# Head norm, first gate tiles and the linear unit's gate tiles in a float32 hybrid block on one Trainium2 core

## The chip, the cores and the metric

One core of a Trainium2 chip runs the whole program. Its engines work side by side and wait for each other by semaphores: TensorE (PE, with its weight loads PEld) multiplies, VectorE (DVE) and ScalarE (ACT) do the elementwise work, GpSimd (POOL) a little of it, SyncE (SP) issues most transfers. The metric is the time of one execution on the device in microseconds (us).

## What is computed

The reference is a hybrid block followed by two more layers, for 512 positions and a width of 1024, in float32. Here only the first block matters. Its mixer normalises x once and feeds the result to four branches and four sets of gates:

```python
h = rms_norm(x, norm_mix)                       # x * rsqrt(mean(x*x)) * w
rw = h @ w_in[rwkv]                             # RWKV branch, a recurrence over positions
o = head_norm(o, 64e-5) * ln_w + ln_b           # per head of 64: subtract mean, divide by deviation
y_rwkv = (o + bonus) * gate
y_lru = h_scan * gelu(gate_in)                  # linear recurrent unit
branch = einsum('bsmw,mwd->bsmd', ys, w_branch)
merged = sum(sigmoid(gate_logits) * branch)
```

## The kernel before, in words

Everything lies transposed: 128 features on the partitions, 512 positions along the row. So a vector of 1024 features is eight tiles of 128x512. A float32 product is made of three fp32r products: each operand is split into a high part (written by ACT) and a low part (the difference, written by DVE). One weight tile of 1024 by 128 makes one output tile in a `proj` of 8 x 3 = 24 matmuls (lines 622 to 624). The raw weight comes by a transfer that SP issues, ACT writes `whi` (line 1328), DVE writes `wlo` (line 2052). There are three raw slots and three split slots (`NRAW`, `NSPL`), and `W.ahead` splits weights up to three tiles ahead of the tile named in `hi(...)` on ACT or `lo(...)` on DVE: `hi("lg", 0)` splits the weights of `lg` tile 3, and that needs `lg` tile 0 to be finished, since it takes that tile's slot.

Each engine has a program of its own, in an order written out by hand; there is no planner. `due(...)` gives the semaphore values to wait for, and an instruction that waits holds up all behind it on its engine. Seven PSUM banks go round in a ring (`bank`, `PS.free`); an eighth, `PL`, takes the small sums.

Stages of the first block, in order: `rw` (RWKV projections, with the norm's root in `km`), `chunks` (the recurrence in 8 chunks), `post` (head norm and output of RWKV), the norm of x once more (`hn`, for all later tiles), `merge(3)` (gate tiles g and branch tiles b of RWKV in turn: g0, g1, b0, g2, b1, ...), `mamba`, `merge(0)`, `lru`, `merge(1)`, `ret`, `merge(2)`, and so on.

In `post`, PE makes for each tile j the head mean (`ym`, line 834), the bonus (`yb`, line 838) and the sum of squares (`yc_sum`, line 829). DVE subtracts the mean (line 2326) and multiplies the bonus (line 2330). ACT squares (line 1522), takes the root (line 1525), DVE inverts it (line 2334), ACT and DVE split it into `VR` (lines 1528 and 2337). Then for each j PE spreads the root (`yv`, line 844) and makes the gate (`yg`, line 848), and DVE makes three operations (lines 2341, 2345, 2348) that end in the output tile Yt[j].

All engines' `end po` comes next. Then `hn`: ACT squares x (line 1338), PE sums it (line 640), ACT takes the root (line 1344), DVE inverts it (line 2067) and scales (line 2075), ACT writes the high parts (line 1352), DVE (line 2061) and for every third tile POOL (line 3114) the low parts. The x tiles had been overwritten by `rw` and `chunks`, so SP loads them again after the recurrence (line 3206). Then `merge(3)`: ACT copies the eight output tiles to `yp` (line 1546), DVE writes their low parts, and PE starts g0.

In `lru`, PE makes eight `lx` tiles with their block products (line 946) and then eight `lg` tiles. ACT runs tanh and exp for all eight tiles (lines 1663 and 1666), then eight roots (line 1670), then `hi("lg", j)` and the gelu of `lg` tile j. DVE runs three operations per tile (lines 2530 to 2536), then for each tile a product and a scan (lines 2540 and 2543), then `lo("lg", j)` (line 2052) and the output product (line 2548).

Of the kernel before, what the change touches and what calls it, by code (L numbers as in the profile page):

```python
# [310 lines left out]
def build(nc, T, known=None):  # L311

    with ExitStack() as ctx:
# [41 lines left out]
        PT, CT, DP, X = sb(ctx, "PT", NPAR), sb(ctx, "CT", NCON), sb(ctx, "DP", 62), sb(ctx, "X", 8 * S)  # L355
# [22 lines left out]
        with ExitStack() as c1:  # L378
            VF, BSF, SG, H2 = sb(c1, "VF", 8 * S), sb(c1, "BS", S), sb(c1, "SG", S), sb(c1, "H2", 1024)
            PC = sb(c1, "PC", 64)  # L380
            VFt, PC3, BSR, H2R = tiles(VF), r3(PC, 8), BSF.bitcast(F32R), H2.bitcast(F32R)
# [17 lines left out]
            with ExitStack() as c2:  # L399
                yc, sqt = tiles(sb(c2, "yc", 8 * S)), tiles(sb(c2, "sqt", 4 * S))  # L400
                G2, VRF = sb(c2, "G2", 1024), sb(c2, "VR", S)
                VRR = VRF.bitcast(F32R)
# [6 lines left out]
        with ExitStack() as c1:  # L409
            rtmp = tiles(sb(c1, "rtmp", 6 * S))  # L410
# [87 lines left out]

        def norm_of(tag, n, buffers, xs, wname, w0, outs, after=()):
            return dict(tag=tag, n=n, sq=buffers[0:2], r=buffers[2], sc=buffers[3:], xs=xs, w=(wname, w0), outs=outs,  # L500
                        after=list(after))

        def lo_key(tag, j):
# [7 lines left out]


        N = {
            "hn": norm_of("hn", 8, rtmp, Xt, "norm_mix", 0, H, ends("po")),
        }

# [88 lines left out]
        def tensor_program(pe):  # L605
# [29 lines left out]
            def ss(nm, j):  # L635
                tag, n = nm["tag"], nm["n"]
                b = bank("ss", tag, hold=True) if j == 0 else PS.slots[PS.at["ss", tag]]
                for s in due("pe", ("act", "sq", tag, j), ("con", "ld")):
                    pe.wait_ge(*s)
                MM(b, C("ones"), nm["sq"][j % 2], start=(j == 0), stop=(j == n - 1)).then_inc(*up("pe", "ss", tag, j))  # L640
                if j == n - 1:
                    PS.let("ss", tag)

# [178 lines left out]
            def post():  # L822
# [3 lines left out]
                def yc_sum(j):  # L826
                    for s in due("pe", ("act", "ysq", j), ("dve", "bs")):
                        pe.wait_ge(*s)
                    MM(PL[0:16, :], C("selsum", 16 * j, 16 * j + 16), sqt[j % 4], start=(j == 0),
                       stop=(j == 7)).then_inc(*up("pe", "ysq", j))  # L830

                for j in range(8):
# [6 lines left out]
                yc_sum(7)  # L839
                for j in range(8):  # L840
                    b = bank("yv", j)
                    for s in due("pe", ("dve", "vr")):
                        pe.wait_ge(*s)
                    MM(b, heads2(j), VRR, start=True, stop=True).then_inc(*up("pe", "yv", j))
# [10 lines left out]
            def merge(m):  # L855
                hn, st = h_of("hn"), "m%d" % m
                tile((st, "g", 0), "w_gate", (m, 0), 8, H, hn)
                for j in range(8):
                    if j < 7:
                        tile((st, "g", j + 1), "w_gate", (m, j + 1), 8, H, hn)  # L860
# [5 lines left out]
            def mamba():  # L866
                hn = h_of("hn")
# [70 lines left out]
            def lru():  # L938
                hn = h_of("hn")
# [18 lines left out]
            def ret():  # L958
                hn = h_of("hn")
# [360 lines left out]
        def scalar_program(act):  # L1320
# [13 lines left out]
            def square(nm, j, *keys):  # L1334
                tag = nm["tag"]
                for need in due("act", *keys, ("pe", "ss", tag, j - 2) if j >= 2 else None):
                    act.wait_ge(*need)
# [708 lines left out]
        def vector_program(dve):  # L2046
# [307 lines left out]
            def merge(m):  # L2354
# [23 lines left out]
                for j in range(8):  # L2378
                    if j < 7:
                        lo(st, "g", j + 1)  # L2380
# [970 lines left out]
```

## Time and profile before

| | us |
|---|---|
| median of three runs | 4041.46 |
| the three runs | 4040.36, 4041.46, 4042.90 |
| the profiled execution, its own time | 4038.73 |
| its span | 4036.9 |

| engine | busy us | share of the span |
|---|---|---|
| PE | 3785.7 | 94% |
| PEld | 3047.2 | 75% |
| DVE | 2170.1 | 54% |
| ACT | 1501.6 | 37% |
| POOL | 108.1 | 3% |

A timeline row gives the start in us, the duration, the engine, the line, the operation, its output and inputs, how many instructions are merged in the row, and in brackets how long the engine had been idle and which instruction released it. A row of the table of stretches gives the busy time of each engine in a stretch of the span, the clock granted to TensorE as a share of full speed (PEclk; 1.00 is 2.4 GHz and 0.50 is 1.2 GHz), and the transfers. One float32 matmul stands in the trace as two records.

### The profile page before, as it was taken

To read this page: it belongs to the slowest core of one execution; us is meant where nothing else is said; L and a number is where in the kernel's file an instruction comes from. 1 tells how busy PE (TensorE), PEld (TensorE's weight loads), DVE (VectorE), ACT (ScalarE), POOL (GpSimd) and SP (SyncE) were. 2 spreads that over 40 slices of the span, in tenths; PEclk is the share of its full clock that TensorE was granted. 3 is DMA by queue.
4 is the path that set the end of the run, shared out by engine and by line. 5 is a ranking of instruction groups with operands and counts; after the bars stand their busy time and mean duration, and the time that the engine had idled before them with its cause. 6 is when DMAs were issued, how large, how long until landed. Compare 5 with 4: busy or idle time off the path is not lost.

```text
span 4036.9 us, 52064 instructions
## 1 busy us (share of the span) xinstructions
PE 3785.7 (94%) x22086; PEld 3047.2 (75%) x22086; DVE 2170.1 (54%) x3218; ACT 1501.6 (37%) x2563; POOL 108.1 (3%) x134
## 2 busy tenths in 40 slices
PE   8888799889899999999989999999999999999998
PEld 6578478776677678777877787888777778878886
DVE  6854536555542457476565544434575554454345
ACT  5733234234322334243355423322433553232233
POOL 0022000100000000000001000000000010000000
PEclk9999899899999999999999999999999999999999
DMA  3100122012231122323300132332332002322322
GB/s 137 58 3 3 43 84 100 32 59 78 84 115 63 63 89 88 97 86 96 109 9 14 48 96 93 98 96 91 90 107 75 1 16 79 97 94 90 103 87 80
DMA packets 90812, 297.52 MB, mean 74 GB/s; under 512 B 10067, under 2 KB 12627, under 8 KB 90196
## 3 DMA queue, kind: packets, MB, share of 16 engines
q1 hardware_dynamic: 88704, 286.50, 22.2%
q10 hardware_dynamic: 1876, 7.71, 0.5%
q8 instruction: 173, 2.83, 0.3%
q14 instruction: 59, 0.48, 0.0%
HBM read 292.07 MB, written 2.10 MB: 73 GB/s over the span
## 4 chain that ended last, share of the span: by engine, by line
PE 81%; DVE 12%; ACT 5%; issue 1%; POOL 1%; DMA 0%; SPq 0%; DVEq 0%; ACTq 0%
PE ps L622 20%; PE ps L623 20%; PE ps L624 20%; PE ps L1173 3%; PE ps L1192 3%; DVE wlo L2052 2%; ACT whi L1328 2%; PE ps L1183 2%; DVE ftm L2087 1%; PE ps L766 1%; PE ps L759 1%; PE ps L657 1%; PE ps L771 1%; PE ps L659 1%; PE ps L658 1%
## 5 line engine op out<-in xcount | busy, mean ns | idle before, releaser
L2052 DVE TENSOR_TENSOR wlo<-wraw,whi 128x1024 fp32r<-128x1024 f32 (+5 forms) x603 | 664.2, 1103 | 1306.6 <-ACT whi L1328 1300.1
L1328 ACT ACTIVATE whi<-wraw 128x1024 fp32r<-128x1024 f32 (+5 forms) x603 | 578.1, 959 | 1308.3 <-PE ps L624 1225.6
L622 PE MATMUL ps<-HH,whi 128*128 128x512 f32 x1816 | 723.9, 399 | 32.3 <-DVE wlo L2052 18.9
L623 PE MATMUL ps<-HL,whi 128*128 128x512 f32 x1816 | 711.1, 392 | 0.0
L624 PE MATMUL ps<-HH,wlo 128*128 128x512 f32 x1816 | 710.8, 391 | 0.0
L622 PEld LDWEIGHTS ps<-HH,whi 128*128 128x128 f32 x1816 | 343.5, 189 | 117.2 <-issue 24.7
L623 PEld LDWEIGHTS ps<-HL,whi 128*128 128x128 f32 x1816 | 343.6, 189 | 76.8 <-issue 6.3
L624 PEld LDWEIGHTS ps<-HH,wlo 128*128 128x128 f32 x1816 | 343.3, 189 | 72.3
L622 PE MATMUL ps<-HBh,whi 128*128 128x512 f32 x752 | 297.7, 396 | 6.8 <-DVE HBl L2615 6.3
L624 PE MATMUL ps<-HBh,wlo 128*128 128x512 f32 x752 | 293.6, 390 | 0.0
L623 PE MATMUL ps<-HBl,whi 128*128 128x512 f32 x752 | 293.5, 390 | 0.0
L622 PEld LDWEIGHTS ps<-HBh,whi 128*128 128x128 f32 x752 | 141.6, 188 | 41.0 <-DVE HBl L2615 8.9
L623 PEld LDWEIGHTS ps<-HBl,whi 128*128 128x128 f32 x752 | 141.6, 188 | 31.2 <-issue 1.9
L624 PEld LDWEIGHTS ps<-HBh,wlo 128*128 128x128 f32 x752 | 141.5, 188 | 29.8
L1173 PE MATMUL ps<-KPALL,ZT 128*128 128x256 f32 (+3 forms) x384 | 140.2, 450 | 22.7 <-DVE VT L2881 7.8
L622 PE MATMUL ps<-act2h,whi 128*128 128x512 f32 x384 | 152.4, 397 | 0.0
L623 PE MATMUL ps<-act2l,whi 128*128 128x512 f32 x384 | 152.2, 396 | 0.0
L624 PE MATMUL ps<-act2h,wlo 128*128 128x512 f32 x384 | 152.2, 396 | 0.0
L2893 DVE TENSOR_REDUCE sm<-ps 128x1 f32<-128x256 f32 (+3 forms) x192 | 87.1, 455 | 101.0 <-PE ps L1175 99.9
L622 PE MATMUL ps<-yph,whi 128*128 128x512 f32 x256 | 99.6, 389 | 0.0
L623 PE MATMUL ps<-ypl,whi 128*128 128x512 f32 x256 | 99.6, 389 | 0.0
L624 PE MATMUL ps<-yph,wlo 128*128 128x512 f32 x256 | 99.6, 389 | 0.0
(639 smaller groups left out, 6498.1 us busy)
## 6 DMA issues: line engine op xcount, KB each, us to landing
wraw<-in_w_ff SPq DMA_DIRECT2D x88, 512.0 KB, 3.5
wraw<-in_w_bg SPq DMA_DIRECT2D x48, 512.0 KB, 3.5
wraw<-in_ffn_up SPq DMA_DIRECT2D x44, 512.0 KB, 3.2
wraw<-in_w_z SPq DMA_DIRECT2D x36, 512.0 KB, 3.2
wraw<-in_w_gate SPq DMA_DIRECT2D x32, 512.0 KB, 3.2
wraw<-in_w_br SPq DMA_DIRECT2D x32, 512.0 KB, 3.3
wraw<-in_w_rw SPq DMA_DIRECT2D x26, 512.0 KB, 3.3
wraw<-in_w_mam SPq DMA_DIRECT2D x24, 512.0 KB, 3.2
```

Of the source, the lines that this page charges most:

```text
L622: MM(b[0:m, :], hi[:, k, c0:c0 + m], x[0], start=(start and k == 0), stop=False)
L623: MM(b[0:m, :], hi[:, k, c0:c0 + m], x[1], start=False, stop=False)
L624: ins = MM(b[0:m, :], lo[:, k, c0:c0 + m], x[0], start=False, stop=(stop and k == n - 1))
L657: MM(b[:, 0:cols], x[0][:, cs], hi[:, k, 0:cols], start=first, stop=False)
L658: MM(b[:, 0:cols], x[1][:, cs], hi[:, k, 0:cols], start=False, stop=False)
L659: ins = MM(b[:, 0:cols], x[0][:, cs], lo[:, k, 0:cols], start=False, stop=end)
L1173: MM(b[:, 0:nk], job["q"](h)[:, qs], job["k"](h)[:, k0:k0 + nk], start=True, stop=False)
L1183: ins = TR(b[:, 128 * kb:128 * kb + 128], job["pb"][i % 3][:, 128 * kb:128 * kb + 128], C("ident"))
L1192: ins = MM(ob[:, 64 * h:64 * h + 64], job["pt"][i % 3][:, 128 * kb:128 * kb + 128], job["v"](h, kb), start=(kb == 0), stop=(kb == nkb - 1))
L1328: ACTV(W.pair_of(n)[0], W.raw_of(n), ACT.Copy).then_inc(*up("act", "whi", n))
L2052: TT(l, W.raw_of(n), h.bitcast(F32), SUB).then_inc(*up("dve", "wlo", n))
L2893: RED(s[:, h:h + 1], PS.of("sc", *key)[:, 0:job["nk"]], AXX, ALU.max, negate=True).then_inc(*(up("dve") if x else up("dve", "mx", *key)))
```

## The change

1. The inverse root of x's norm, which `rw` has in `km`, is turned onto the partitions by four transposes after projection 6 (PE) and copied to four columns of `DP` (DVE). At the start of `post` four products with the identity spread it over a held bank `hr`. The squares, sums, root and inverse of `hn` are gone, and so is POOL's part.
2. DVE scales x (`hn_scale`) and writes the low parts (`hn_lo`) inside the loop of `post` over ym and yb; ACT writes the high parts (`hn_hi`) there.
3. x is loaded again in two halves, the first after chunk 6, the second after chunk 7.
4. PE makes gate tile g0 of `merge(3)` between the two loops of `post`, and g1 inside the second loop, ahead of j = 2. ACT makes both gates' sigmoids before it copies any output tile; DVE writes the low part of output tile j-1 in step j, and splits two weight tiles in steps 1 and 3.
5. The root of the head norm is split in place in `BS` instead of `VR`, and three square buffers do instead of four.
6. In `lru`, gelu is written to the output tile; the first three `hi`/gelu come before the eight roots, `lo` of `lg` stands in DVE's loops (after j = 3 and 7 of the first, after each odd j of the second).

```diff
@@ tensor program
+                    if i == 6:
+                        b = bank("hrt")
+                        for s in due("pe", ("dve", "rc")):
+                            pe.wait_ge(*s)
+                        for c in range(4):
+                            ins = TR(b[:, 16 * c:16 * c + 16], km[0:16, 128 * c:128 * c + 128], C("ident")[0:16, 0:16])
+                        ins.then_inc(*up("pe", "hrt"))
...
+                b = bank("hr", hold=True)
+                for s in due("pe", ("dve", "hrt")):
+                    pe.wait_ge(*s)
+                for c in range(4):
+                    ins = MM(b[:, 128 * c:128 * c + 128], DP[:, 62 + c:63 + c].to_broadcast([128, 128]), C("ident"),
+                             start=True, stop=True)
+                ins.then_inc(*up("pe", "hr"))
...
                 yc_sum(7)
-                for j in range(8):
+                gate_tile(3, 0)
+                PS.let("hr")
+                for j in range(8):
+                    if j == 2:
+                        gate_tile(3, 1)
                     b = bank("yv", j)
...
-                for j in range(8):
-                    ss(N["hn"], j)
-                here("pe", "end", "hn")
@@ scalar program, post and merge
+                    ACTV(sqt[j % 3], yc[j], ACT.Square).then_inc(*up("act", "ysq", j))
+                    if j >= 2:
+                        hn_hi(j - 2)
...
+                hn_hi(6)
+                hn_hi(7)
+                for need in due("act", ("dve", "vri"), ("pe", "yb", 7)):
+                    act.wait_ge(*need)
+                ACTV(BSR[0:16, :], sqt[0][0:16, :], ACT.Copy).then_inc(*up("act", "vrh"))
...
+                if m == 3:
+                    for j in range(2):
+                        hi(st, "g", j)
+                        sigmoid(j)
                 for need in due("act", *ends(before)):
@@ scalar program, lru
+                def gelu(j):
+                    hi("lg", j)
+                    evac(("lg", j), Yt[j], ACT.Gelu_apprx_tanh, ("lgg", j))
+
+                for j in range(3):
+                    gelu(j)
                 for j in range(8):
                     for need in due("act", ("dve", "lt", j)):
                         act.wait_ge(*need)
                     ACTV(lt[j], lt[j], ACT.Sqrt).then_inc(*up("act", "ls", j))
...
+                for j in range(3, 8):
+                    gelu(j)
@@ vector program, rw and post
+                    if j == 5:
...
+                        VCP(DP[:, 62:66], r3(PS.of("hrt")[:, 0:64], 16)[:, :, 0]).then_inc(*up("dve", "hrt"))
...
+                    if j >= 2:
+                        hn_scale(j - 2)
...
+                    if j >= 3:
+                        hn_lo(j - 3)
+                hn_scale(6)
+                hn_scale(7)
+                PS.free(("hr",), ("dve", "sc", "hn", 7))
+                hn_lo(5)
...
                 REC(sqt[0][0:16, :], sqt[0][0:16, :]).then_inc(*up("dve", "vri"))
...
+                hn_lo(6)
+                hn_lo(7)
...
+                TT(BSR[32:48, :], sqt[0][0:16, :], BSF[0:16, :], SUB).then_inc(*up("dve", "vr"))
...
+                    if j:
+                        result_lo(3, j - 1)
+                    if j in (1, 3):
+                        lo("m3", "g", j // 2)
+                result_lo(3, 7)
@@ vector program, lru
                     TS(lt[j], lt[j], 2.0 ** -116, None, MAXOP).then_inc(*up("dve", "lt", j))
+                    if j in (3, 7):
+                        lo("lg", j // 4)
...
                     SCAN(xc[j], ra[j], iu[j], 0.0, MUL, ADD).then_inc(*up("dve", "lh", j))
...
+                    if j % 2:
+                        lo("lg", 2 + j // 2)
+                for j in range(8):
+                    if j >= 6:
+                        lo("lg", j)
+                    for need in due("dve", ("act", "lgg", j), ("dve", "lh", j)):
+                        dve.wait_ge(*need)
+                    TT(Yt[j], xc[j], Yt[j], MUL).then_inc(*up("dve", "ly", j))
@@ sync program
-                    sp.dma_start(X, T["x"]).then_inc(*up("xr", "ld", by=16))
+                    for i in range(2):
+                        for need in due("sp", ("pe", "O", 6 + i)):
+                            sp.wait_ge(*need)
+                        sp.dma_start(X[:, 4 * S * i:4 * S * i + 4 * S],
+                                     T["x"][:, 4 * S * i:4 * S * i + 4 * S]).then_inc(*up("xr%d" % i, "ld", by=16))
```

## Rows read from the trace of the kernel before

**Rows 1.** Table of stretches: the two places, busy us and PEclk.

```profile
441.00:526.00 85.00, 61.98 (x153) 29.82 (x152) 53.17 (x68) 26.83 (x41) 2.53 (x2) 0.80 0.16 62
...
1011.50:1030.00 18.50, 0.15 (x2) 0.15 (x1) 18.03 (x22) 7.35 (x10) 0.00 (x0) 0.63 0.00 0
```

**Rows 2.** Timeline of PE from the head norm to merge tile g2.

```profile
458.25 1.03 PE L829 MATMUL psl<-sqt,CT 128*16 128x512 f32 x2
...
465.15 0.76 PE L844 MATMUL ps<-VR,H 128*128 128x512 f32 x1 [5.87 <-DVE VR L2337]
...
484.88 10.22 PE L640 MATMUL ps<-rtmp,CT 128*128 128x512 f32 x16 [7.77 <-ACT rtmp L1338]
501.54 0.77 PE L622 MATMUL ps<-HH,whi 128*128 128x512 f32 x1 [6.43 <-DVE HL L2061]
...
525.97 0.39 PE L622 MATMUL ps<-HH,whi 128*128 128x512 f32 x1
```

**Rows 3.** Timeline of DVE in the same stretch.

```profile
454.60 0.69 DVE L2326 SCALAR_TENSOR_TENSOR yc<-ps,YS 128x512 f32<-128x512 f32 x1 [0.17 <-PE ps L834]
...
456.84 0.69 DVE L2326 SCALAR_TENSOR_TENSOR yc<-ps,YS 128x512 f32<-128x512 f32 x1 [0.17 <-PE ps L834]
...
460.22 3.34 DVE L2334 RECIPROCAL sqt<-sqt 16x512 f32<-16x512 f32 x1 [1.31 <-ACT sqt L1525]
...
476.75 0.69 DVE L2348 TENSOR_TENSOR YS<-yc,ps 128x512 f32<-128x512 f32 x1
...
478.92 0.69 DVE L2348 TENSOR_TENSOR YS<-yc,ps 128x512 f32<-128x512 f32 x1
...
503.36 1.41 DVE L2075 SCALAR_TENSOR_TENSOR rtmp<-X,PT,rtmp 128x512 f32<-128x512 f32 x2
...
514.72 4.91 DVE L2061 TENSOR_TENSOR ypl<-YS,yph 128x512 fp32r<-128x512 f32 x8 [0.74 <-ACT yph L1546]
```

**Rows 4.** Timeline of ACT in the same stretch.

```profile
458.22 1.28 ACT L1525 ACT_TABLE_LOAD   x1
459.51 0.68 ACT L1525 ACTIVATE sqt<-psl,DP 16x512 f32<-16x512 f32 x1
...
521.10 1.05 ACT L1328 ACTIVATE whi<-wraw 128x1024 fp32r<-128x1024 f32 x1
522.04 0.59 ACT L1358 ACTIVATE ga<-ps 128x512 f32<-128x512 f32 x1
```

**Rows 5.** Timeline of PE in the mamba stage: the forms nearest to the added ones.

```profile
733.05 0.39 PE L876 MATMUL ps<-CT,AC 16*128 16x16 f32 x4
...
740.04 3.74 PE L899 MATMUL ps<-AC,CT 128*128 128x128 f32 x32
```

**Rows 6.** Timeline of PE in the linear unit: the wait ahead of lg tile 3.

```profile
1029.88 0.77 PE L622 MATMUL ps<-HH,whi 128*128 128x512 f32 x1 [18.35 <-DVE wlo L2052]
```

**Rows 7.** Timeline of ACT in the linear unit.

```profile
1007.48 1.28 ACT L1670 ACT_TABLE_LOAD   x1
...
1037.32 1.06 ACT L1328 ACTIVATE whi<-wraw 128x1024 fp32r<-128x1024 f32 x1 [17.07 <-PE ps L624]
...
1059.08 1.06 ACT L1328 ACTIVATE whi<-wraw 128x1024 fp32r<-128x1024 f32 x1 [3.89 <-PE ps L624]
```

**Rows 8.** Timeline of DVE in the linear unit.

```profile
1005.38 0.43 DVE L2536 TENSOR_SCALAR ltt<-ltt 128x512 f32<-128x512 f32 x1
...
1014.50 1.22 DVE L2543 TENSOR_TENSOR_SCAN lxc<-lra,liu 128x512 f32<-128x512 f32 x1
...
1028.53 1.20 DVE L2052 TENSOR_TENSOR wlo<-wraw,whi 128x1024 fp32r<-128x1024 f32 x1
```

**Rows 9.** Table of stretches: the clock across two idle times of PE.

```profile
459.00:465.00 6.00, 0.28 (x1) 0.00 (x0) 4.01 (x2) 1.80 (x3) 0.00 (x0) 0.86 0.00 0
...
985.00:990.00 5.00, 1.84 (x5) 0.53 (x3) 3.56 (x5) 2.99 (x4) 0.00 (x0) 0.90 0.28 93
```

**Rows 10.** Transfers from 400 to 560 us: issue, KB, us to landing.

```profile
X<-in_x SPq DMA_DIRECT2D x1, 2048.0 KB, 8.7
```

More of the change, by code:

```diff
@@ L398, in build @@
                     NC_, Xj, P1, RS, ST, STn = (sb(c2, n, 512) for n in ("NCc", "Xj", "P1", "RSs", "ST", "STn"))
[L399 to L402, printed above, removed]
+            sb(c1, "below", 51 * S)
+            VF, BSF, SG, H2 = sb(c1, "VF", 8 * S), sb(c1, "BS", S), sb(c1, "SG", S), sb(c1, "H2", 1024)
+            PC = sb(c1, "PC", 64)
+            VFt, PC3, BSR, H2R = tiles(VF), r3(PC, 8), BSF.bitcast(F32R), H2.bitcast(F32R)
+        with ExitStack() as c1:
+            sb(c1, "below", 16 * S)
+            rtmp, G2, sqt = tiles(sb(c1, "rtmp", 4 * S)), sb(c1, "G2", 1024), tiles(sb(c1, "sqt", 3 * S))
+            sb(c1, "below", 18 * S)
+            yc = tiles(sb(c1, "yc", 8 * S))
         def heads2(j):
@@ L1332, in hi @@
                     split_hi(n)
[L1334 to L1337, printed above, removed]
-                ACTV(nm["sq"][j % 2], nm["xs"][j], ACT.Square).then_inc(*up("act", "sq", tag, j))
-            def root(nm):
-                tag, n = nm["tag"], nm["n"]
-                for need in due("act", ("pe", "ss", tag, n - 1), ("dve", "dp")):
-                    act.wait_ge(*need)
-                ACTV(nm["r"], PS.of("ss", tag), ACT.Sqrt, scale=1.0 / (128 * n), bias=EPSC).then_inc(*up("act", "rt", tag))
-                PS.free(("ss", tag), ("act", "rt", tag))
-            def scaled_hi(nm):
-                for j in range(nm["n"]):
-                    sc = nm["sc"]
-                    for need in due("act", ("dve", "sc", nm["tag"], j)):
-                        act.wait_ge(*need)
-                    ACTV(nm["outs"][j][0], sc[j % len(sc)], ACT.Copy).then_inc(*up("act", "hi", nm["tag"], j))
             def evac(key, dst, fn, mark, rows=128, cols=S, **kw):
@@ L1549, in merge @@
                              scale=P("ssm_norm", j)).then_inc(*up("act", "hi", st, j))
-                def sigmoid(j):
-                    for need in due("act", ("dve", "ga" if m == 3 else "mt", st, j - 2) if j >= 2 else None):
-                        act.wait_ge(*need)
-                    evac((st, "g", j), ga[j % 2], ACT.Sigmoid, ("ga", st, j))
-                hi(st, "g", 0)
-                sigmoid(0)
+                if m != 3:
+                    hi(st, "g", 0)
+                    sigmoid(0)
                 if m == 0:
@@ L1568, in merge @@
                 for j in range(8):
-                    if j < 7:
+                    if j < 7 and (m != 3 or j):
                         hi(st, "g", j + 1)
@@ L1670, in lru @@
                     ACTV(lt[j], lt[j], ACT.Sqrt).then_inc(*up("act", "ls", j))
-                for j in range(8):
-                    hi("lg", j)
-                    for need in due("act", ("dve", "lh", j)):
-                        act.wait_ge(*need)
-                    evac(("lg", j), lt[j], ACT.Gelu_apprx_tanh, ("lgg", j))
+                for j in range(3, 8):
+                    gelu(j)
                 here("act", "end", "lr")
@@ L2020, in scalar_program @@
             post()
-            merge(3, "hn")
+            merge(3, "ch")
             mamba()
@@ L3155, in gpsimd_program @@
             here("pool", "end", "po")
-            scaled(N["hn"])
-            here("pool", "end", "hn")
             here("pool", "end", "m3")
```

126 lines of the change are left out of this document (45 added, 81 removed).

## The prediction

> **What bounds the kernel now.** The page comes first: PE is busy 94% of the span, so whatever saves time must close an idle time of PE or take work off it. The table of stretches says where PE is idle. From 441 to 526 us it is busy for 61.98 of 85 us and runs at 0.80 of its clock; from 1011.5 to 1030 it is busy for 0.15 of 18.5 us while DVE is busy for 18.03 [rows 1]. The timelines then say what it waits for. In the first stretch the last sum of squares starts at 458.25, the head root's spread at 465.15 after 5.87 us idle, the sums of the norm of x at 484.88 after 7.77, gate tile g0 at 501.54 after 6.43; g0, g1 and b0 follow, and g2 starts at 525.97 [rows 2]. In the second, PE has done `lg` tiles 0 to 2 and waits 18.35 us for the `wlo` of tile 3 [rows 6], which stands behind ACT's eight roots and DVE's eight scans, though nothing in it needs them. So two marks are enough for the sum: the start of g2 in `merge(3)`, and the end of `lg` tile 7 at 1059.08, where ACT is released for its next split [rows 7]. Behind each PE runs tile after tile, so a shift of the mark is a shift of the end.
>
> **Small added work.** Four transposes stand in the projections of `rw`, where PE is dense: the same form, four in a row, takes 0.39 us with its tail [rows 5]; bounds 0.1 and 0.4, taken 0.3. DVE's copy of four columns hides in DVE's slack there; if it did not, it would cost less than the shortest DVE row, 0.43 [rows 8]. The spread of the root stands on the path, ahead of the first head mean: four float32 products are eight records, and 32 records of the same form take 3.74 us [rows 5], so 8/32 of that, 0.9 us (to 1.8 at the lower clock).
>
> **Post, first loop.** Before, PE sets the pace: the subtractions of the mean start at 454.60 and 456.84, 2.24 apart [rows 3]. After, DVE has four operations per step from j = 3 on: mean 0.61, scale 0.67 (two in a row take 1.41, less the tail of 0.74), bonus 0.61, low part 0.61 (eight in a row take 4.91) [rows 3], together 2.5. DVE becomes the bound by 0.25 a step, 1.1 us up to the last mean, which then starts at 456.84 + 0.9 + 1.1 = 458.9. From its start on, the mean, three scales, a bonus and two low parts take 4 x 0.61 + 3 x 0.67 = 4.4 us: 463.3. ACT meanwhile squares (0.6, as the sigmoid of the same size [rows 4]), makes a high part (0.6), loads its table (1.28) and takes the root (0.68) [rows 4]: 459.6 + 3.2 = 462.8. So the inverse starts at 463.3 instead of at 460.22, and takes 3.34 [rows 3]: 466.7. The low parts 6 and 7 (1.3) and the low part of the root (0.7) follow: the root is ready at 468.7, against some 465.0 before (PE takes it up at 465.15 [rows 2]). **This loop costs 3.7 us.** In it g0 runs: PE is free at 461.3, and its last three products start when the last low part is there, at 468.0, so g0 ends at 468.8, just as the root is ready. It costs nothing.
>
> **Post, second loop.** DVE starts at about 469.5. A step costs 2.17 us (478.92 less 476.75 [rows 3]); after steps 0 and 1 it is 473.8. Now comes the new wait. DVE's low part of output tile 0 needs ACT's high part, and ACT stands in the sigmoid of g1 first. PE does two steps' products (2.2 us) and then g1. A tile takes (1059.08 - 1037.32) / 4 = 5.44 us [rows 7], so g1 ends at 476.5; ACT splits a weight (0.94 to the next start) and does the sigmoid (about 0.5) [rows 4] and the copy (0.6): 478.7. DVE is idle 4.9 us, and queued behind it are all its outputs, so PE's branch tile b0 waits too. From 478.7: eight low parts (4.9), six steps (13.0), two weight splits (2.3): 499. The last product group of b0 takes 1.3 us at the lower clock: **g2 starts at 500.4, not at 525.97**: 25.6 us earlier. The next tile starts at the lower clock, though. In the linear unit the first tile after the wait took 1037.32 - 1029.88 = 7.44 us, 2.0 more than the others [rows 6, 7]; before, g0 paid that. Less 2.0 here and the 0.3 in `rw`: 23.3 us.
>
> **The x loads.** SP has two transfers instead of one, and behind them on its queue only the weights of `merge(3)`, which go out after chunk 7 as before. The whole 2048 KB landed 8.7 us after the issue [rows 10]. The second half goes out as `post` begins, at about 441, and is needed at about 456 by the scale of tile 4: hidden with 7 us in hand. The first half runs beside chunk 7.
>
> **Linear unit.** ACT is free at 1007.48 [rows 7]. It splits the weight of `lg` 3 by 1008.5. DVE asks for it after j = 3, at 1005.8 [rows 8], and waits 2.7 us; `wlo` is there at 1009.8, before PE has ended tile 2 at 1011.5 (1029.88 less 18.35 [rows 6]). The 18.35 us are gone. What is late next is `lg` 4: DVE does four tiles of three operations, 2.0 each (from 1005.8 to the product ahead of the first scan, at 1013.8 [rows 8]), then the split of 1.2: 1019.0, against the end of tile 3 at 1017.0. PE waits 2.0 us. Then DVE needs two scans with their products and one split per tile: (1028.53 - 1014.50 + 0.6) / 8 = 1.83 each [rows 8], so 3.7 + 1.2 = 4.9, under PE's 5.44. Tiles 4 to 7 run through, and tile 7 ends at 1019.0 + 4 x 5.44 = 1040.8. The three gelus ahead of the roots add a table load on ACT, 1.28 [rows 4]; the roots end at about 1018.8, in step with DVE, and gelus 3 to 7 then run beside the tiles. The mark moves from 1059.08 to 1040.8: 18.3 us. If the 2 us of waiting bring the clock down, 1 to 2 us are lost: I take 0.8. **17.5 us.**
>
> **Sum.** 23.3 + 17.5 = 40.8 us. The profiled execution took 4038.73 (span 4036.9), which gives 3997.9 for one like it; the median stands 2.7 above it, at 4041.46, which gives 4000.7. I take 4001.
>
> **A rule weighed.** Around ACT's change of function the trace shows the load at 458.22 for 1.28 us and the root at 459.51, with nothing between [rows 4]. The Trainium skill, page ScalarE: Activation LUTs, section What ACT_TABLE_LOAD costs, gives a drain of about 1380 ns beside a load of about 1283 ns. By that page the head root would be ready 0.9 us later than DVE is, and the sum would be an estimated 0.9 us smaller; the row shows the load alone, and I go by the row.
>
> **Rivals.**
> - *The lower clock through the output loop.* In the idle time that began at 459.3 [rows 2], PE's clock was halved for the last 1.7 of six us (a mean of 0.86), and in the one that began at about 986.8 (1.84 us of work behind 985) for the last 1.0 of five (0.90) [rows 9]: idle for 4 us, and for 2. After the change PE waits about 2 us inside g0. If it falls there and stays low, g0 takes 2.7 us longer, the first two steps' products 2.2 and g1 5.4, and the whole chain through ACT's sigmoid with them: about 10 us, 4011. Against it: g1 is dense, and the tile after the linear unit's wait lost 2.0 us only [rows 6, 7]. The Trainium skill, page TensorE: Matmul & The Clock Gate, Part 1, says that the throttled state is the default and activity releases it; by that rule this loss is real but short.
> - *DVE in the first loop doesn't overlap with ACT.* If each low part waits for its high part, 0.6 us and the signals around it, the loop costs up to 8 x 0.7 = 5.6 us more: 4006. Against it: each low part comes a whole step after its high part is asked for.
> - *The linear unit's gain goes to a new wait.* If DVE's stall for `lg` 3 and the five later splits fall behind the tiles, each tile waits. At one more us a tile it is 5 us: 4006.
> - *Slower.* The second half of x lands late: the scale of tile 4 waits for it, and DVE, in order, holds the whole of `post`. The price is its landing less 456; from a landing at about 497 on, 56 us behind its issue, the change makes the kernel slower. The whole of x took 8.7 us [rows 10], so a half should take 4.4; at the 62 GB/s that the stretch averaged [rows 1] it takes 17 and costs 2 us; it would have to take thirteen times the row's. At fifteen times, 66 us, it is 51 us late: 4052.
> - *It does not do what it says*: the root of `rw` is the same quantity, and both moved pieces of work have no input that comes later, so I give this no more than the 2% for no change, in which both new waits (DVE behind g1, PE behind `lg` 4) would have to eat all.
>
> **How the numbers follow.** The sum with its terms within their bounds, 3993 to 4006: 0.80. The lower clock, 4011 with 4006 to 4016: 0.10. DVE or the linear unit losing more, alone or together, to 4016: 0.05. No change 0.02, slower 0.03. The range of 8 in 10, with the added work at its bounds and the lower clock taken in at its low end: 3992 to 4013. What a measurement of this kernel can tell from no change is about 0.2%, 8 us, so faster means under 4033: 0.95; same 0.02; slower 0.03.
>
> **What would show it.** In the trace of after: POOL's part gone; PE's first output product at about 469 and the split of `lg` 4 as PE's only wait in the linear unit, of about 2 us; an idle time of DVE of about 5 us ahead of the low part of output tile 0, released by ACT; g2 of `merge(3)` some 60 us behind the start of `post` at 441 instead of 85. Wrong would be: a PE clock of 0.5 through g1, a wait for the x load, a DVE step in the first loop above 2.7 us, or more than 3 us of waiting between `lg` tiles.

## The result and the profile after

The changed kernel took 3995.25 us (median of 4 runs, 3992.37 to 3996.56), the one before 4040.91 (4 runs, 4037.0 to 4042.9): a ratio of 0.9887, 95% interval 0.987 to 0.9904, 45.7 us less. The prediction was 4001 with a range of 3992 to 4013, faster. The profiled execution took 3995.15 with a span of 3993.3, so it stands in the middle of its runs; the one of before, 4038.73, stood 2.2 below its median.

The two places first, as a table of stretches (us of the stretch, busy us of PE, PEld, DVE, ACT and POOL with their instructions, PEclk, DMA share, GB/s):

```profile
441.00:459.00 18.00, 16.54 (x38) 4.37 (x37) 16.21 (x26) 8.51 (x14) 0.00 (x0) 1.00 0.37 154
459.00:480.00 21.00, 18.20 (x67) 12.17 (x66) 14.94 (x19) 9.47 (x13) 0.00 (x0) 1.00 0.00 1
480.00:500.00 20.00, 13.96 (x34) 7.78 (x33) 17.04 (x25) 3.97 (x7) 0.00 (x0) 0.73 0.15 52
500.00:526.00 26.00, 26.00 (x110) 21.35 (x109) 7.85 (x8) 6.08 (x7) 0.00 (x0) 0.94 0.24 81
970.00:990.00 20.00, 18.76 (x83) 15.20 (x81) 15.85 (x26) 19.71 (x30) 0.00 (x0) 1.00 0.07 26
990.00:1010.00 20.00, 18.86 (x77) 15.51 (x77) 19.73 (x21) 7.60 (x10) 0.00 (x0) 0.91 0.31 106
```

Where [rows 1] had 61.98 busy us in 85, at 0.80 of the clock, PE is now busy for 48.70 of 59 us up to 500, and dense from there on. POOL has no part left in `post`. Most of what is still idle stands in the third row, at 0.73 of the clock. In the linear unit the empty stretch of 18.5 us is gone.

The timeline of PE in the first place (start, us, engine, line, out<-in, idle time before it and what ended it) answers to [rows 2]:

```profile
439.19 1.13 PE L824 MATMUL ps<-CT,DP 128*128 128x128 f32 x8 [0.79 <-ACT YS L1491]
...
459.68 0.50 PE L612 MATMUL ps<-HH,whi 128*128 128x512 f32 x1
...
465.63 0.50 PE L612 MATMUL ps<-HH,whi 128*128 128x512 f32 x1 [1.57 <-DVE HL L2053]
...
467.13 0.39 PE L843 MATMUL ps<-BS,H 128*128 128x512 f32 x1
...
468.91 0.80 PE L612 MATMUL ps<-HH,whi 128*128 128x512 f32 x1
...
494.02 0.50 PE L612 MATMUL ps<-yph,whi 128*128 128x512 f32 x1 [1.70 <-DVE ypl L2053]
...
496.79 0.79 PE L612 MATMUL ps<-yph,whi 128*128 128x512 f32 x1 [1.79 <-DVE ypl L2053]
...
499.51 0.63 PE L612 MATMUL ps<-HH,whi 128*128 128x512 f32 x1
```

The spread of the root opens `post`, g0 begins at 459.68 and is ended by three late products, the first output product follows at 467.13 without a wait, g1 begins at 468.91, and g2 starts at 499.51, 60.3 us behind the opening instead of 85.3. At the end b0 takes its last low parts one by one, and the clock falls: the products of 0.39 us take 0.63.

DVE's timeline answers to [rows 3]:

```profile
449.95 0.68 DVE L2312 SCALAR_TENSOR_TENSOR yc<-ps,YS 128x512 f32<-128x512 f32 x1
...
452.41 0.68 DVE L2312 SCALAR_TENSOR_TENSOR yc<-ps,YS 128x512 f32<-128x512 f32 x1
...
461.70 3.33 DVE L2328 RECIPROCAL sqt<-sqt 16x512 f32<-16x512 f32 x1
464.96 1.21 DVE L2053 TENSOR_TENSOR HL<-rtmp,HH 128x512 fp32r<-128x512 f32 x2
466.20 0.68 DVE L2333 TENSOR_TENSOR BS<-sqt,BS 16x512 fp32r<-16x512 f32 x1
...
471.30 0.69 DVE L2344 TENSOR_TENSOR YS<-yc,ps 128x512 f32<-128x512 f32 x1
477.15 0.69 DVE L2053 TENSOR_TENSOR ypl<-YS,yph 128x512 fp32r<-128x512 f32 x1 [5.17 <-ACT yph L1539]
...
496.05 1.47 DVE L2053 TENSOR_TENSOR ypl<-YS,yph 128x512 fp32r<-128x512 f32 x2
```

A step of the first loop takes 2.46 us from j = 4 on and DVE is not idle in it: DVE is the bound. The inverse has no wait in front of it any more (1.31 us before). Then there is the new wait of 5.17 us, released by ACT's high part of output tile 0. ACT's timeline shows why it came late, and its table load answers to [rows 4]:

```profile
459.34 1.28 ACT L1513 ACT_TABLE_LOAD   x1
460.64 0.68 ACT L1513 ACTIVATE sqt<-psl,DP 16x512 f32<-16x512 f32 x1
...
475.06 1.06 ACT L1328 ACTIVATE whi<-wraw 128x1024 fp32r<-128x1024 f32 x1 [4.70 <-PE ps L614]
476.02 0.58 ACT L1338 ACTIVATE ga<-ps 128x512 f32<-128x512 f32 x1
476.50 1.14 ACT L1539 ACTIVATE yph<-YS 128x512 fp32r<-128x512 f32 x2
```

ACT is idle for 4.70 us until g1 has ended, splits a weight, does g1's sigmoid, and only then copies output tiles 0 and 1, of which the second had been there since 472.0. In the linear unit PE's, ACT's and DVE's timelines answer to [rows 6 to 8]:

```profile
991.14 0.76 PE L612 MATMUL ps<-HH,whi 128*128 128x512 f32 x1 [2.38 <-ACT ltt L1665]
...
998.21 0.39 PE L612 MATMUL ps<-HH,whi 128*128 128x512 f32 x1
```

```profile
998.47 1.06 ACT L1328 ACTIVATE whi<-wraw 128x1024 fp32r<-128x1024 f32 x1 [4.58 <-PE ps L614]
...
1003.91 1.06 ACT L1328 ACTIVATE whi<-wraw 128x1024 fp32r<-128x1024 f32 x1 [3.90 <-PE ps L614]
...
1014.79 1.06 ACT L1328 ACTIVATE whi<-wraw 128x1024 fp32r<-128x1024 f32 x1 [3.90 <-PE ps L614]
```

```profile
980.71 1.23 DVE L2044 TENSOR_TENSOR wlo<-wraw,whi 128x1024 fp32r<-128x1024 f32 x1 [2.63 <-ACT whi L1328]
...
989.78 1.22 DVE L2044 TENSOR_TENSOR wlo<-wraw,whi 128x1024 fp32r<-128x1024 f32 x1
```

PE's only wait there is the 2.38 us ahead of `lg` 4. The profile names ACT's roots as its releaser, but these had ended at 991.03 and nothing of theirs enters the tile; the last thing the tile needs is DVE's `wlo`, which ends at 991.00. From its first product to that of `lg` 5, `lg` 4 then takes 998.21 - 991.14 = 7.07 us instead of 5.44, which is 1.6 us more. (ACT's splits, at 998.47 and 1003.91, stand at the ends of tiles, 0.26 us behind the next tile's first product.)

**The span in five stages.** All kernels were cut at the same five marks: the first gram product of the chunks, PE's first product of `post`, tile b1 of `merge(3)`, the last block product of the linear unit, and the first product in `ret` that is not part of a projection tile (line 965 of before and after). So "linear unit" also holds `merge(1)` and the first tiles of `ret`, which are the same in all kernels. The columns "post" and "linear unit" hold the change; the three others hold the same instructions in every kernel, and "untouched" is their sum (with the stretch ahead of the chunks left out, 203.5 us in before and 203.7 in after).

| kernel | chunks | post | middle | linear unit | rest | untouched |
|---|---|---|---|---|---|---|
| before | 237.2 | 90.7 | 462.0 | 163.3 | 2880.2 | 3579.4 |
| before_again | 235.8 | 89.5 | 461.0 | 163.3 | 2880.9 | 3577.7 |
| after | 235.5 | 67.4 | 459.1 | 146.8 | 2880.8 | 3575.4 |
| control | 235.6 | 66.1 | 461.1 | 146.8 | 2878.1 | 3574.8 |
| lru_only | 239.2 | 90.9 | 462.0 | 146.9 | 2875.3 | 3576.5 |
| post_only | 235.5 | 66.0 | 457.7 | 164.4 | 2882.2 | 3575.4 |
| root_only | 235.5 | 63.5 | 460.0 | 164.2 | 2874.9 | 3570.4 |
| root_lru | 235.7 | 63.5 | 460.1 | 146.9 | 2881.4 | 3577.2 |
| order_g1 | 237.8 | 61.9 | 459.3 | 146.6 | 2880.7 | 3577.8 |
| g0_within | 235.6 | 57.7 | 459.8 | 146.7 | 2877.8 | 3573.2 |
| x_whole | 235.7 | 66.2 | 461.0 | 146.9 | 2878.7 | 3575.4 |
| lulo_only | 235.0 | 64.7 | 461.2 | 142.7 | 2878.7 | 3574.9 |
| g0_lulo | 235.5 | 57.6 | 461.5 | 143.2 | 2880.7 | 3577.7 |

The change saved 23.3 us in `post` and 16.5 in the linear unit, 39.8 together. The untouched stages vary by several us from one trace to the next, in both directions, and so between kernels whose medians are compared. That is why each experiment below is read from the stage that it touches first, and from its median second. A stage is not free of this either: `post` holds the same instructions in after, control, post_only, x_whole and lulo_only, and took 67.4, 66.1, 66.0, 66.2 and 64.7 us. The start of g2, one tile before the end of that stage, repeats better: 60.3, 60.1, 60.3, 60.0 and 59.2 us behind the opening. The linear unit repeats within 0.3 us (146.6 to 146.9).

### The profile page after: what moved, and what is told of

It reads as the page before. It is cut to its first block, busy times and chain, and to the rows that moved or that the text cites. A ratio compares the mean times of both kernels' runs of the same rounds, so it can differ in the third digit from the quotient of the medians.

```text
span 3993.3 us, 52039 instructions
## 1 busy us (share of the span) xinstructions
PE 3773.1 (94%) x22082; PEld 3043.1 (76%) x22082; DVE 2163.7 (54%) x3219; ACT 1497.0 (37%) x2555; POOL 104.9 (3%) x132
## 4 chain that ended last, share of the span: by engine, by line
PE 81%; DVE 12%; ACT 5%; issue 1%; POOL 1%; DMA 0%; SPq 0%; DVEq 0%; ACTq 0%; POOLq 0%
PE ps L612 20%; PE ps L614 20%; PE ps L613 20%; PE ps L1173 3%; PE ps L1192 3%; DVE wlo L2044 2%; ACT whi L1328 2%; PE ps L1183 2%; DVE ftm L2060 1%; PE ps L754 1%; PE ps L638 1%; PE ps L747 1%; PE ps L759 1%; PE ps L640 1%; PE ps L639 1%
```

## The experiments

My theory: two independent gains, `post` some 23 us and the linear unit some 17, and what remains is set by DVE's order (the wait behind g1). The rivals: the gains are of another size or depend on one another; gate tiles in `post` are what brings the gain, or only the early root; the x load sets something; and the rest of the 45.7 us is not the change at all.

### One half at a time

`lru_only` is the kernel before with the linear unit of the change; `post_only` is the change with the linear unit of before. The diff is that part of the change's own diff; its core:

```diff
-                for j in range(8):
-                    hi("lg", j)
-                    for need in due("act", ("dve", "lh", j)):
-                        act.wait_ge(*need)
-                    evac(("lg", j), lt[j], ACT.Gelu_apprx_tanh, ("lgg", j))
+                for j in range(3, 8):
+                    gelu(j)
```

> The kernel before with the change in the linear unit alone (gelu to the output tiles, the first three ahead of the roots, the low parts of the weights in DVE's loops). Theory: the two places are independent, and this one moves the end of lg tile 7 by 18.35 us of waiting less 2.4 us of new waiting ahead of lg tile 4, so 16.5 us faster than before, 4024 (ratio 0.996). Rival: the 45.7 us of the whole change owe several us to the places of the half-clock stretches in other stages (chunks, mamba), and each half of the change brings such us too; then this one gives 19 or more or 13 or less.

> The changed kernel with the linear unit as it was before. Theory: 24 to 27 us faster than before, 4015 (ratio 0.994), and its gain and that of the linear unit alone add up to that of the whole, 45.7 us. Rival: the sum of both falls short of the whole by more than 3 us, and the rest is not owed to the waits taken away.

Measured: `lru_only` 4019.49 us beside 4039.19 of before, ratio 0.9955 (0.9942 to 0.9967), 19.7 less; `post_only` 4019.26, ratio 0.9954 (0.9941 to 0.9968), 19.9 less. By the medians both expectations missed, and both came out on the side of the rivals: `lru_only` gained over 19, and the two halves together 39.6, which is 6.1 short of the 45.7. By the stages they came out as the theory had them. In the table the stage that each touches is that of the full change (146.9 and 146.8; 66.0 and 66.1 in `control`) and the other is that of before, so the gains are independent: 16.5 and 24.7, 41.2 together, against 39.8 for the change. The medians put the halves nearly level: `post_only`'s runs lie widely apart (4011.35 to 4020.80) and its profiled one was the shortest, and `lru_only`'s untouched stages were 2.9 us shorter than those of before. I read the halves by the stages; why the whole beats the sum of the medians is not shown.

### The early root without the gate tiles

`root_only` is `post_only` with g0 and g1 back where every other merge has them, behind the output loop, on all engines:

```diff
-                gate_tile(3, 0)
                 PS.let("hr")
                 for j in range(8):
-                    if j == 2:
-                        gate_tile(3, 1)
                     b = bank("yv", j)
...
-                if m != 3:
-                    gate_tile(m, 0)
+                gate_tile(m, 0)
...
-                    if j in (1, 3):
-                        lo("m3", "g", j // 2)
                 result_lo(3, 7)
```

> As the run before, and gate tiles g0 and g1 of merge 3 go back behind the loops (their sigmoids behind the copies of the output tiles, DVE's weight splits behind its low parts): the early root alone. Theory: DVE sets the pace of the output loop at 2.78 us a step and has no wait of 5.2 us and no weight splits in it, so it ends near 489; g0 and g1 then run beside its end and behind it, and g2 starts 3 us later than with the gates within: 21 to 22 us faster than before, 4019. Rival: the gates within are worth the two tiles that they take out of the way, 10.9 us, and the root alone gives 14 us, 4027.

Measured: 4011.79 us, ratio 0.9933 (0.9921 to 0.9945): faster than `post_only`, where I had expected slower. `root_lru`, the same edit on the full change, was run beside the change itself (`control`, its exact copy):

> The changed kernel as it is, for comparison on one chip with the three that follow. Theory: 0.9885 of the kernel before, some 45 us faster; g2 of merge 3 starts 60 us behind the first product of the output stage's start, whatever the length of the stages ahead of it. Rival (the clock's share): the stages that the change does not touch differ by several us between two executions of this same kernel, since the stretches at half clock lie elsewhere; then the mark in the trace repeats within 0.5 us and the total does not within 2 us.

> The changed kernel with gate tiles g0 and g1 of merge 3 back behind the output loop (as in the root alone, with the linear unit's change). Theory, from the traces of the root alone: g1 inside the output loop holds up DVE by 5.2 us and two weight splits by 2.3 more, while behind the loop g0 and g1 are hidden by DVE's own tail, three steps of it; so this is 2.6 to 3.9 us faster than the changed kernel up to branch tile b1, 3991. Rival: the 7.5 us between the medians of the two earlier runs are real, and it is 7 to 8 us faster, 3987.

Measured: `control` 3993.50, ratio 0.9887 (0.9871 to 0.9902), which repeats the ratio of the change, and its g2 starts 60.1 us behind the opening; `root_lru` 3991.62, ratio 0.9881 (0.9863 to 0.9898). Both pairs agree in the stage: 63.5 against 66.0 and 66.1, so b1 starts 2.6 us earlier with the gate tiles outside. The medians of the first pair lie 7.5 us apart, those of the second 1.9. The profiled spans of the first (4009.6 and 4001.8) are 7.8 apart, of which `post` has 2.6, the rest stage 7.3 (2882.2 and 2874.9) and the middle -2.3: most of it isn't the edit. So **the two gate tiles within `post`, as the change places them, gain nothing and cost some us**. How many is not sharp: against 63.5 in both kernels without them stand 64.7 to 67.4 in the five traces with them, and g2 starts 59.2 to 60.3 us behind the opening instead of 58.1; the runs of the second pair overlap. The whole gain of the first place comes from the rest, that is from the early root and the scaling of x moved into the loop. PE's timeline of `root_only` shows all its waits from 462 to 512 us:

```profile
467.00 0.76 PE L840 MATMUL ps<-BS,H 128*128 128x512 f32 x1 [7.28 <-DVE BS L2320]
...
478.02 0.49 PE L840 MATMUL ps<-BS,H 128*128 128x512 f32 x1 [0.38 <-DVE YS L2331]
479.28 1.12 PE L844 MATMUL ps<-SG,G 128*128 128x512 f32 x2 [0.77 <-DVE yc L2324]
480.79 0.50 PE L612 MATMUL ps<-HH,whi 128*128 128x512 f32 x1 [0.38 <-DVE YS L2331]
```

PE waits 7.28 us for the root, but DVE then goes through its outputs with waits of 0.95 and 0.24 us in the first step alone. DVE has three outputs and four low parts more to do when PE has finished the last output product; PE does g0 and g1 in that time, from 480.79 on, and b0 finds its low parts ready. I had expected g2 3 us later than in the change, which is at some 502.5; it started at 497.24. The two tiles fit beside DVE's tail, and I had let part of them stand behind it. In the change the tiles save PE's time, of which there is enough, and cost DVE's, of which there is none: 5.2 us of wait and two splits of 1.15 us each.

### The order around g1

`order_g1` keeps both tiles within and lets ACT copy outputs 0 and 1 before it turns to g1; PE does g1 one step later:

```diff
-                    if j == 2:
+                    if j == 3:
                         gate_tile(3, 1)
...
-                    for j in range(2):
-                        hi(st, "g", j)
-                        sigmoid(j)
+                    hi(st, "g", 0)
+                    sigmoid(0)
...
                         ACTV(yp[j][0], Yt[j], ACT.Copy).then_inc(*up("act", "hi", st, j))
+                        if m == 3 and j == 1:
+                            hi(st, "g", 1)
+                            sigmoid(1)
```

> The changed kernel with two places exchanged: ACT copies output tiles 0 and 1 ahead of the split and sigmoid of gate tile g1, and PE makes g1 ahead of output step 3 instead of 2. Theory: DVE's wait of 5.2 us for the copy of output tile 0 is on the path of b0 and goes away with nothing in its place, 4 to 5 us faster than the changed kernel, 3991, 50 us faster than before. Rival: the wait comes back at the next output step, where DVE waits for the products that stand behind g1 on PE, and nothing or under 2 us is gained, 3994 to 3995.

Measured: 3989.35 us, ratio 0.9881 (0.9868 to 0.9895), against 3993.5 to 3995.3 for the change, which was measured at other times: 4 to 6 less, and 49.8 under the kernel before of its own measurement where the change was 45.7 and 46.2 under its own. The stage is 61.9 instead of 64.7 to 67.4, and g2 starts 55.1 us behind the opening instead of 59.2 to 60.3. DVE's timeline at the place of the wait:

```profile
473.67 0.69 DVE L2346 TENSOR_TENSOR YS<-yc,ps 128x512 f32<-128x512 f32 x1
474.28 0.68 DVE L2055 TENSOR_TENSOR ypl<-YS,yph 128x512 fp32r<-128x512 f32 x1
474.88 1.22 DVE L2046 TENSOR_TENSOR wlo<-wraw,whi 128x1024 fp32r<-128x1024 f32 x1
```

The wait of 5.17 us is gone and nothing has taken its place; the gain is the wait. It was on the path, as the prediction had it.

### Only g0 within

`g0_within` joins the two findings. g0 stays between the loops, where PE waits for the root anyway; g1 goes behind the loop, and DVE's splits for both go behind the low parts:

```diff
                 for j in range(8):
-                    if j == 2:
-                        gate_tile(3, 1)
                     b = bank("yv", j)
...
-                    if j < 7 and (m != 3 or j):
+                    if j < 7:
                         gate_tile(m, j + 1)
...
-                    if j in (1, 3):
-                        lo("m3", "g", j // 2)
```

> The changed kernel with g0 alone between the two loops (in the time in which PE waits for the head root) and g1 behind the output loop; DVE's weight splits stand behind its low parts. Theory: g0 costs nothing where it stands and g1 is hidden by DVE's tail, b0 ends just behind the last low part, at about 491.5 on the trace's clock, g2 starts 7.7 us earlier than in the changed kernel: 7 to 9 us faster than it, 3987. Rival: b0 waits for its last inputs, the clock falls, and g2 and b1 run at half speed for 3 to 4 us; then the gain is 5 us, 3990.

Measured: 3985.61 us, ratio 0.9866 (0.9851 to 0.9882), 7.9 less than `control` on the same chip. The table of stretches (its columns as above):

```profile
441.00:459.00 18.00, 16.55 (x38) 4.37 (x37) 16.05 (x26) 8.36 (x14) 0.00 (x0) 1.00 0.39 158
459.00:480.00 21.00, 16.92 (x50) 8.56 (x48) 19.94 (x27) 9.45 (x13) 0.00 (x0) 1.00 0.00 1
480.00:500.00 20.00, 19.61 (x87) 16.09 (x87) 15.16 (x20) 6.57 (x9) 0.00 (x0) 1.00 0.24 79
```

PE is busy for 53.08 of 59 us (48.70 in the change) and the clock doesn't fall. DVE is busy for 19.94 of the 21 us from 459 on, instead of 14.94. g2 starts 52.2 us behind the opening, 7.8 us earlier than in `control`. g0 costs nothing here, as the prediction said; g1 is hidden in DVE's tail. The comparison with `root_lru`, measured beside it, gives the worth of g0 alone: 57.7 us in the stage instead of 63.5, and 3985.61 instead of 3991.62. So g0 between the loops saves 6 us, and it is g1 inside the loop, with DVE's two splits, that takes this and more away again.

### The split ahead of `lg` 4

DVE's two splits among the four-operation tiles go after j = 4 and 6 instead of 3 and 7, once on the change (`lulo_only`) and once on `g0_within` (`g0_lulo`):

```diff
-                    if j in (3, 7):
-                        lo("lg", j // 4)
+                    if j in (4, 6):
+                        lo("lg", j // 2 - 2)
```

> The changed kernel with DVE's splits for lg weights 3 and 4 behind tiles 4 and 6 of its first loop in the linear unit, and nothing else. Theory, from the run with both edits: PE's wait of 2.4 us ahead of lg tile 4 and the half-clock stretch behind it (1.9 us) go, and the stage is 3.5 to 4 us shorter from the last block product to the ret stage. Rival: the 3.5 us between the two traces before came from the clock at the stage's start alone.

> As the run before, and in the linear unit DVE's splits of lg weights 3 and 4 stand behind tiles 4 and 6 of its first loop instead of 3 and 7. Theory: DVE's wait for ACT falls from 2.6 to about 0.6 us and the split for lg 4 is there before PE asks, so PE's wait of 2.4 us and the 1.9 us at half clock behind it go: 4 us faster than the run before, 3983. Rival: the next split (lg 5) becomes late by as much, since DVE needs 4.9 us a tile against PE's 5.4 and has no lead, and under 2 us are gained.

Measured: `lulo_only` 3988.71 us, ratio 0.9879 (0.9864 to 0.9894), 5 to 6.5 less than the change; `g0_lulo` 3983.39, ratio 0.9862 (0.9846 to 0.9878), where the median is only 2.2 under `g0_within` and the runs overlap. The stage is 142.7 and 143.2 instead of 146.8, that is 4.1 and 3.6 less: the wait of 2.38 us and what the clock took behind it, 7.07 - 5.44 = 1.6. (`g0_lulo` shows less because its first `lg` tile, at half clock behind an earlier wait, ended later: `lg` 1 starts 7.2 us behind the last block product instead of 6.5 in `g0_within`.) DVE's wait shrinks from 2.63 us to

```profile
979.18 1.23 DVE L2044 TENSOR_TENSOR wlo<-wraw,whi 128x1024 fp32r<-128x1024 f32 x1 [0.62 <-ACT whi L1328]
...
984.29 1.22 DVE L2044 TENSOR_TENSOR wlo<-wraw,whi 128x1024 fp32r<-128x1024 f32 x1
```

and PE has no wait between the tiles, so the split of `lg` 5, which the rival had late, is there in time. `g0_lulo` is the fastest kernel of the study, 56.3 us under before and some 10 to 12 under the change.

### The x loads

`x_whole` issues both halves of x only after chunk 7, which takes away the early half:

```diff
                 if n == again:
+                    for need in due("sp", ("pe", "O", 7)):
+                        sp.wait_ge(*need)
                     for i in range(2):
-                        for need in due("sp", ("pe", "O", 6 + i)):
-                            sp.wait_ge(*need)
```

> The changed kernel with both halves of x loaded after chunk 7. Theory: the first scale of x stands 5 us behind that point and a half lands some 4.4 us after its issue, so DVE waits for at most 2 us in the third step, and part of that is taken up in the steps that PE paces: 0 to 2 us slower than the changed kernel. Rival (the slower case of the prediction, a late landing holds DVE): if the transfers beside the loop take two or more times as long as alone, the wait is 5 us or more and the whole stage shifts by it.

Measured: 3994.99 us, ratio 0.9894 (0.9878 to 0.9911), the change's own time. The wait of up to 2 us that I had thought possible is not there: "post" is 66.2 as in `control`, and DVE has no wait for x. The transfers, grouped (issue, KB, median us to landing), from 425 us on, first of `x_whole` and then of the change, where only the second half falls in that stretch:

```profile
X<-in_x SPq DMA_DIRECT2D x2, 1024.0 KB, 6.8
```

```profile
X<-in_x SPq DMA_DIRECT2D x1, 1024.0 KB, 4.9
```

Even two halves behind each other are there when the scales need them. The second half alone, at 4.9 us where the slower rival needed 56, never came near to harm.

### The rest of the difference

The stages of the change account for 39.8 us of the 45.7. Was the rest a change in the kernel, or the spread of the untouched stages? The kernel before, traced once more:

> The kernel before, traced once more. Theory: the 4 to 5 us by which the whole change beats the sum of its two places are the clock's: the untouched stages (the recurrence, merge 3's second tile to the linear unit's last block product, and all behind the linear unit) add up to 3579 us in the first trace of before and 3575 in both of the changed kernel, and this trace differs from the first by 2 us or more. Rival: it repeats within 1 us, and the change speeds up the untouched stages by some cause that the two places do not show.

Measured: 4036.98 us, and the untouched stages are 3577.7 instead of 3579.4. The difference of 1.7 us lies between what the two theories expected, and decides for neither. All traces together say more. The untouched stages are 3570.4 to 3577.8 in eleven traces of changed kernels, 3575.3 in the mean, and 3577.7 and 3579.4 in the two of before: one of before lies within the spread, one 1.6 us above it. The 5.9 us that the two stages leave of the 45.7 are, then, 2.1 from the profiled run of before, which stood below its median, and 4.0 from the untouched stages of that trace, less the 0.2 ahead of the chunks. Measured against the mean of the changed kernels the untouched stages of before are 2.4 and 4.1 longer; with two traces of before, whether some of this is a side effect of the change or all of it spread is left open. The second trace also has 89.5 us in `post` instead of 90.7.

## Why the prediction was right, step by step

- **Small added work: right.** The spread opens `post` and is eight records; the first head mean starts 0.97 us behind it (forecast 0.9). The chunks begin at 203.7 instead of 203.5 us (forecast 0.3); in other traces with the transposes they begin at 203.3 to 205.1, so the trace does not tell this term from the spread.
- **First loop: right.** (`post` opens at 440.7 in before and at 439.2 in after; times are given from there.) From j = 4 on a step takes 2.46 us (forecast 2.5), the one of j = 3 2.60, and DVE is the bound. The inverse starts 22.5 us behind the opening of `post` (forecast 22.6), the root is ready at 27.7 (28.0), g0 ends at 27.9 (28.1). The loop is indeed slower than before, and pays for itself by what it no longer has behind it.
- **The wait behind g1: right in place and size**, 5.17 us (forecast 4.9), released by ACT as said, and on the path, as `order_g1` showed. (The terms that the prediction gives for ACT add up to 478.5, not to its 478.7; a slip of 0.2.) What I had not drawn from it is that the tile which causes it, g1, costs more than it brings: the prediction compared with before only, and there it could be counted as part of a gain.
- **g2 60.3 us behind the opening (forecast 59.7).** DVE's last low part ends 58.3 us behind it, just as forecast. The 0.6 came after it: PE had two groups of three products left, not one, and both ran at the half clock, 2.7 us instead of 1.3.
- **The half clock at the next tile: right in this trace, with luck.** g2 took 7.07 us up to b1 at 506.58, 1.6 over a dense tile (taken 2.0). In the four other traces with the same instructions it took 0.6 (`control`), 0.3 (`post_only`), 0.7 (`x_whole`) and nothing (`lulo_only`) over one. So the stage's gain of 23.3 lies so near the forecast (25.6 - 2.0 = 23.6) because of the traces taken; any of the five against either trace of before gives 22.1 to 26.0.
- **The rival of a lower clock through the output loop did not come about.** PE idled 1.57 us within g0, and the clock of 459 to 480, with g1 in it, stayed at 1.00. It did fall later in the loop, to a mean of 0.73 from 480 to 500, where DVE sets the pace; up to the start of g2 this cost the 0.6 us above.
- **Linear unit: right in the mechanism, 1.0 too high.** DVE waited 2.63 us for the split of `lg` 3 (forecast 2.7) and the 18.35 us were gone. What counts of PE's new wait is when it ends, and this is set by DVE: `lg` 4 was to start 25.6 us behind the last block product and started 25.5 behind it. The wait was 2.38 us instead of 2.0 only because PE came to it earlier: `lg` 1 started 6.6 us behind the last block product instead of 7.1. Mis-sized is the clock: it took 1.6 us, not the 0.8 that I took as a middle of "1 to 2, if at all". Another 0.3 was a mistake in the frame: I added tiles of 5.44, which are counted from end to end, to the start of a tile, and `lg` 7 ends 0.26 us behind that. (For the same reason the 2.0 us lost behind the wait of before are 1.7.) The stage gave 16.5 against 17.5.
- **The sum.** 39.8 against 41.1 by the two stages (23.6 and 17.5, without the 0.3 for `rw`, which stands ahead of them); the difference between the medians was 45.7. The missing piece is no step of the sum but its frame: that the untouched 3575 us would be the same to the microsecond. The table shows that they are not. That the time still lies in the range is not owed to a term that foresaw these 5 to 6 us: the low end had been set by the bounds of other terms.
- **The rule weighed.** In the trace of after the load takes 1.28 us at 459.34 and the root starts at 460.64, with nothing between. Any further time of ACT's would have shown here, since DVE took the root up at 461.70, 0.4 us after it was done. By the Trainium skill (ScalarE: Activation LUTs, What ACT_TABLE_LOAD costs), which adds a drain of about 1380 ns to the load, the inverse would have started an estimated 1 us later; the trace disagrees, and the measurement decides. On the clock, the Trainium skill (TensorE: Matmul & The Clock Gate, Part 1) has activity release the throttle. The trace agrees: behind the waits of b0 and of `lg` 4 PE works without a pause, its products take 0.63 us at first, and they are back at 0.39 within the tile.

## What to carry to other kernels

Work moved into another engine's idle time has to be counted on every engine that it passes. A matmul tile in a loop that DVE sets brings DVE's splits and ACT's activation with it, and an in-order ACT that waits for the tile holds up what DVE needs next. Place it where PE waits anyway (g0 ahead of the root), or behind the loop, where DVE's tail hides it. When halves of a change are weighed, compare a stage between marks rather than the whole time: a whole kernel moved by several us in stages that nobody had touched. Know the spread of the stage too: the same instructions of `post` took 64.7 to 67.4 us in five traces, so one pair of traces does not settle 2 us there.

## What the hardware showed that I had not expected

- **The length of a short idle time does not say here whether the clock falls behind it.** Ahead of `lg` 4 it always did: in seven traces PE waited 1.88 (`lru_only`) to 2.55 us (`order_g1`), and the tile then took 6.9 to 7.2 us instead of 5.44, nearly as much as behind the 18.35 us of before (7.2). The 1.57 us within g0 left the clock at 1.00. In the output loop the same waits came out both ways. A pair of products behind idle times of 0.21, 0.38 and 0.76 us, first in `g0_within` and then in `g0_lulo`, which has the same instructions up to there:

```profile
476.22 1.12 PE L845 MATMUL ps<-SG,G 128*128 128x512 f32 x2 [0.76 <-DVE yc L2334]
```

```profile
476.04 1.89 PE L845 MATMUL ps<-SG,G 128*128 128x512 f32 x2 [0.76 <-DVE yc L2334]
```

  Behind 1.23, 0.38 and 0.76 us such a pair took 2.07 us in after and 1.13 in `control`, which is the same kernel. What decides it was not tested. But the last of the waits that a change leaves is dear: 2.4 us ahead of `lg` 4 cost 4.1.
- **The untouched stages are not constant.** The same instructions took 235.0 to 239.2 us in the chunks and 2874.9 to 2882.2 in the rest stage, in both directions and with no order by kernel. In the chunks the granted clock moves with it (0.96 in the longest, 239.2 us, 0.97 in the two next, 0.98 in all others). That the clock alone makes the difference was not tested.
